# Convolution accumulated in PSUM banks, and key sums placed between the k steps of the next projection block

## The reference

```python
kk = _heads(k * lp['kk'])
kk = kk / jnp.maximum(jnp.sqrt(jnp.sum(kk * kk, axis=-1, keepdims=True)), 1e-12)
```

```python
def conv_mixer(h, w_in, conv_w, w_out):
    gate_b, gate_c, u = jnp.split(h @ w_in, 3, axis=-1)
    return (gate_b * conv3_centred(gate_c * u, conv_w)) @ w_out
```

## Time and profile before

| | |
|---|---|
| median of 3 runs | 1692.13 us (1690.88 to 1695.77) |
| the profiled execution | 1693.48 us |
| its span, first to last instruction | 1691.7 us |
| mean granted TensorE clock | 0.966 |
| TensorE, VectorE, ScalarE, GpSimd busy | 93%, 42%, 33%, 51% |

### The profile page before, as it was taken

The page is one execution under the profiler, slowest core; times in us unless marked ns, Lnnn a source line. Parts: engine busy times, 40 slices in busy tenths (PEclk is TensorE's granted clock), DMA queues, the critical chain, the costliest instruction groups (busy, mean ns, idle before and its releaser), DMA issues. The chain is left out here.

```text
span 1691.7 us, 35349 instructions
## 1 busy us (share of the span) xinstructions
PE 1577.7 (93%) x15550; PEld 1295.6 (77%) x15550; DVE 709.5 (42%) x1113; ACT 565.7 (33%) x811; POOL 862.2 (51%) x404
## 2 busy tenths in 40 slices
PE   4899999988888889999999999999989999999996
PEld 2688868767676777878888888878867788888885
DVE  1433256657676764673121212660295611112135
ACT  3523256533434332333231413233222422222230
POOL 0532204096958570546878788844442544444441
PEclk9999899978999999999999999989989999999998
DMA  7322001022313131224444433312221222222221
GB/s 322 129 75 84 1 1 50 2 102 71 117 46 127 39 118 59 75 75 152 147 149 150 148 136 140 123 50 100 99 99 50 75 100 100 100 100 99 97 77 50
DMA packets 23625, 162.26 MB, mean 96 GB/s; under 512 B 2625, under 2 KB 3265, under 8 KB 4801
## 3 DMA queue, kind: packets, MB, share of 16 engines
q1 hardware_dynamic: 21904, 154.09, 25.9%
q10 hardware_dynamic: 1584, 6.13, 0.9%
HBM read 157.71 MB, written 2.10 MB: 94 GB/s over the span
## 5 line engine op out<-in xcount | busy, mean ns | idle before, releaser
L215 POOL TENSOR_TENSOR v<-raw,v 128x1024 fp32r<-128x1024 f32 x154 | 372.7, 2442 | 378.2 <-ACT v L209 378.2
L232 PE MATMUL bank<-hm,v 128*128 128x512 f32 x1680 | 382.3, 389 | 0.0
L232 PEld LDWEIGHTS bank<-hm,v 128*128 128x128 f32 x1680 | 315.3, 188 | 65.5
L232 PE MATMUL bank<-hid,v 128*128 128x512 f32 x1536 | 350.3, 389 | 0.0
L232 PEld LDWEIGHTS bank<-hid,v 128*128 128x128 f32 x1536 | 288.1, 188 | 59.7
L209 ACT ACTIVATE v<-raw 128x2048 fp32r<-128x2048 f32 x77 | 147.5, 1915 | 399.7 <-PE bank L232 385.6
L2363 DVE TENSOR_TENSOR bank<-bank,rl 128x512 f32<-128x512 f32 x64 | 44.7, 699 | 254.6 <-ACT rl L2334 254.6
L1069 POOL TENSOR_TENSOR raw<-raw,cs 128x2048 f32<-128x2048 f32 x24 | 86.6, 3609 | 110.7 <-issue 64.5
L215 POOL TENSOR_TENSOR w<-raw,w 128x1024 fp32r<-128x1024 f32 x20 | 49.3, 2487 | 132.9 <-ACT w L209 132.9
L542 PE MATMUL bank<-h,w 128*128 128x512 f32 x600 | 109.7, 345 | 0.0
L542 PEld LDWEIGHTS bank<-h,w 128*128 128x128 f32 x600 | 94.0, 191 | 15.1 <-issue 1.1
(11 more groups left out here) (393 smaller groups left out, 2427.4 us busy)
## 6 DMA issues: line engine op xcount, KB each, us to landing
raw<-w_in SPq DMA_DIRECT2D x119, 1024.0 KB, 4.9
mraw<-wm_in SPq DMA_DIRECT2D x16, 1024.0 KB, 4.9
raw<-wm_in SPq DMA_DIRECT2D x3, 1024.0 KB, 16.5
xres<-x_in ACTq DMA_DIRECT2D x1, 2048.0 KB, 9.1
yb<-wm_in SPq DMA_DIRECT2D x2, 1024.0 KB, 19.9
mixed_in<-wm_in SPq DMA_DIRECT2D x2, 1024.0 KB, 23.4
xres<-x_in SPq DMA_DIRECT2D x1, 2048.0 KB, 8.1
out_T<-xres ACTq DMA_DIRECT2D x8, 256.0 KB, 2.0
```

Of the source, the lines that this page charges most:

```text
L215: i = nc.gpsimd.tensor_tensor(W[1][n % 2][:, k:k + 4], raw[n % 2][:, k:k + 4], W[0][n % 2][:, k:k + 4].bitcast(F32), SUB)
L232: last = nc.tensor.matmul(bank(b(s, m), 0, hi - lo), W[w][s][:, k, m * P:(m + 1) * P], H[h][:, k, lo:hi], start=(k == 0 and w == h == 0), ...
```

## The change

It has two parts. The key sums leave their place behind block 7 and go into `key_sums(k)`, called behind each k step of the first tile (m = 0) of block 8: steps 0 and 1 do pair 0, groups 0 to 2 and 3 to 5, steps 2 and 3 pair 1, and so on; each waits for `ksq_ready` of its pair, and the last raises `ksum_done`. In the convolution `c` is no longer the SBUF slice but one of banks 4 to 7, in turn (`mixed_at(k)`): scaling, the two additions and the multiplication by gate_b write there and the last three read it, as do ScalarE's rounding and VectorE's remainder. From k = 4 on VectorE waits, ahead of the scaling, until the remainder of tile k - 4 has been computed.

```diff
                             if n == S_MOD - 1 and k == 2:
                                 lora_pieces()
+                            if n == SUM_AT + 1 and m == 0:
+                                key_sums(k)
                         last.then_inc(tile_done[s][m], 1)
+
+                def key_sums(k):
+
+                    p = k // 2
+                    pe.wait_ge(ksq_ready, p + 1)
+                    for g in range(GD // 2 * (k % 2), GD // 2 * (k % 2 + 1)):
+                        at = 2 * (p * GD + g)
+                        i = nc.tensor.matmul(ksum[:, at:at + 2], kkT[:, p, g * P:(g + 1) * P], K("onesh")[:, ::HD],
+                                             start=True, stop=True)
+                    if k == KT - 1:
+                        i.then_inc(ksum_done, 1)
...
-                    if n == SUM_AT:
-                        for p in range(PAIRS):
-                            pe.wait_ge(ksq_ready, p + 1)
-                            for g in range(GD):
-                                at = 2 * (p * GD + g)
-                                last = nc.tensor.matmul(ksum[:, at:at + 2], kkT[:, p, g * P:(g + 1) * P],
-                                                        K("onesh")[:, ::HD], start=True, stop=True)
-                        last.then_inc(ksum_done, 1)
...
+        def mixed_at(k):
+            return bank(4 + k % 4)
+
...
-                nc.vector.tensor_tensor(hc[1][:, k], conv[:, k, :], hc[0][:, k].bitcast(F32), SUB).then_inc(clo_ready, 1)
+                nc.vector.tensor_tensor(hc[1][:, k], mixed_at(k), hc[0][:, k].bitcast(F32), SUB).then_inc(clo_ready, 1)
...
-                c = conv[:, k, :]
-                link(nc.vector.tensor_tensor(u[:, k, 1:T + 1], bank(2 * (n % 2) + k % 2), c, MUL))
+                c = mixed_at(k)
+                link(nc.vector.tensor_tensor(u[:, k, 1:T + 1], bank(2 * (n % 2) + k % 2), conv[:, k, :], MUL))
                 dve.sem_inc(tile_free[n % 2][k % 2], 1)
+                if k >= 4:
+                    dve.wait_ge(clo_ready, k - 3)
                 link(nc.vector.tensor_scalar(c, u[:, k, 1:T + 1], R("cw", KT + k, KT + k + 1), None, MUL))
...
-                    nc.scalar.activation(hc[0][:, k], conv[:, k, :], ACT.Copy).then_inc(chi_ready, 1)
+                    nc.scalar.activation(hc[0][:, k], mixed_at(k), ACT.Copy).then_inc(chi_ready, 1)
```

## The result

The changed kernel took 1669.1 us in the median of 4 runs (1664.85 to 1677.89), beside 1691.51 us for the kernel before (4 runs, 1681.78 to 1695.77). The ratio is 0.9892 with a 95% interval of 0.9857 to 0.9927: 18.3 us faster, between 12 and 24 (the two medians themselves lie 22.4 us apart, inside that interval). The profiled execution took 1667.99 us, with a span of 1666.2 us and a mean clock of 0.974.

What follows compares the result with a forecast made beforehand. TensorE, busy 93% of the span, was taken as the bound, so only its stops and slow clock could pay. Key sums 6.4 + convolution 9.8 = 16.2 us gave 1676 us, range 1671 to 1682.

Steps and rivals of the forecast that it cites:

- The key sums: Block 8's first tile: without the wait and slow clock it takes 13.8 us in place of 20.19, gaining 6.4 us.
- a root that nobody waits for: ScalarE, block 8's first tile: the root delays the evacuation by 0.21 us, with a whole second tile (8.3 us) as cover.
- (d): Block 8's first tile: key sums between products cost as in their slow half; gain 1.3, total 1681 us; chance 0.07.
- (a): Block 8's first tile: the clock falls under the new mixture, to 1.2 GHz; total 1689.7 us; chance 0.05.
- (b): Block 8: the low clock lasts to the block's end, second tile 8.3 us more; total 1698.0 us; chance 0.02.
- The convolution: Convolution's end and output projection: stops and slow clock mostly go, next block at 1265.6 in place of 1275.39, gaining 9.8 us.
- The stops: TensorE in the output projection: waits for VectorE's residuals of tiles 6 and 7 shrink from 7.36 to about 0.8 us.
- The unknown price: Convolution on VectorE: stretching of the scaling into a bank under GpSimd, bounds 0 and 1.8 us, taken as 0.
- (c): Convolution's last tile: GpSimd still stops bank operations; gain 5.2 to 7.6, total 1678 to 1680.5 us; chance 0.10.
- (e): Convolution: stretching stays whole in the banks, dearer scaling makes the last tile 2.1 us later; total 1687.8 us; chance 0.03.
- The sum: Whole kernel: 6.4 + 9.8 = 16.2 us less, giving a forecast of 1676 us.
- One sign: Changed profile, after the projection behind the key sums: all that follows comes about 6 us earlier.

Runs made afterwards that it cites:

- the lump: Changed kernel, but all 24 key sums in one block between the two tiles of block 8, nothing to wait for; ratio to before 0.9942.
- the experiment with two inputs: Changed kernel, but the first addition writes SBUF and the second reads it there, so one operation has two SBUF inputs; ratio to before 0.9945.
- the second profile of before: The kernel of before, unchanged, run and profiled again; ratio to before 0.9993.
- the second of the changed kernel: The changed kernel, with no further edit, run and profiled again; ratio to before 0.9909.

## Why the prediction was right, point by point

**The key sums.** Forecast 13.8 us for the tile, measured 13.75 or 13.76 in the five profiles of the table that have the move. The pieces hold: from one set of sums to the next 1.72 us (168.81 to 180.86 for seven), as 1.04 + 0.68 had it, with no cost for passing from one kind of matmul to the other, squares ready in time, and a root that nobody waits for. Rival (d), each sum at 0.22 us, is out, and so are (a) and (b): the clock stayed at 1.00. They were nearer than their chances said, though. The argument against (a) was that the clock had fallen behind the idling, and the lump shows that it falls behind such sums without any. What kept it up is that the sums are spread.

**The convolution.** Forecast 12.35 us from the projection's first product to the next block, measured 12.56; the last tile's residual was to come 5.2 us behind its `u` (1253.5 to 1258.7) and came 5.27 (1237.25 to 1242.52). The stops were sized at 0.8 us, and the timeline shows 0.38. The 48 products took 4.38 + 7.33 = 11.71 us, where the sum had 11.1 with the last one's latency: it priced them by the 0.227 us of the stage before. So one term was 0.4 us too dear and one 0.6 too cheap, and that the total is off by only 0.2 us is in part luck. The unknown price, the scaling into a bank under GpSimd, was taken as 0 and is: 753 to 755 ns over eight tiles, four of which (1200.07, 1210.89, 1221.77 and 1232.65) start inside a pass of GpSimd. That agrees with the rule of the Trainium skill in "SBUF — State Buffer", section "Who interferes with whom", and the experiment with two inputs bears its other half out. The advice of the Trainium skill in "VectorE: DVE Perf Modes", section "Rules for kernel authors", to copy out of PSUM first, would have led the wrong way here: working in the bank does cost (0.27 us per tile), but with the intermediate in SBUF, as in the kernel before, the stretching is there. Rivals (c) and (e) are out.

**The sum.** 6.4 and 9.8 us were forecast and 6.4 and 9.6 measured in the stages. The time of 1676 was 7 us above the measured median of 1669.1, which lies 2 us below the low end of the range. The ratio puts it at 0.9892 x 1692.13 = 1673.9, inside. The step that was too tight is the range: it took in the prices of the change and left out how much the rest of the program differs from execution to execution, which the profiles put at 1639 to 1658 us. One sign can't be read for the same cause: what follows the projection was to come about 6 us earlier. The first modulation product came at 337.97 us before and 330.77 after, but at 336.28 in the second profile of before and 336.88 in the second of the changed kernel, whose start was 6.0 us longer.

## What to carry to other kernels

Where VectorE works beside GpSimd, count the SBUF inputs of each VectorE operation on the path: an intermediate kept in a PSUM bank takes the second one away. The count alone doesn't clear an operation, as the scaling from SBUF to SBUF was stretched with one input. Here 0.27 us paid on the scaling bought off up to 2.2 us per operation. Small matmuls that a dense stream can carry belong between its steps, behind work that covers their wait; one block of them can cost the clock even without an idle moment. Price a late tail with the clock behind it: of the 9.6 us here, 7.0 were the stop and the rest mostly the slow products after it.

## What the runs showed that was not expected

The clock fell behind 5.4 us of two-column matmuls that followed each other without a gap, to 0.50 between 184 and 186 us, and the products after them lost 1.7 us. Taking VectorE's second SBUF input away shortened GpSimd's own passes too, from 5.65 to 4.82 us for the last one of the stage. And the recurrence, which no experiment touched, took between 268.0 and 286.9 us in nine profiles, with the clock at 0.50 in one execution where another had 1.00; the start, ahead of all that changed, took between 27.5 and 33.7 us.
